# A block recurrence inside a two-layer decoder trunk: the output part of each block is moved and cut up, its last block gets an order of its own, and one norm is shortened

## The reference

```python
def step(S, w_t, k_t, v_t, a_t, b_t, r_t):          # RWKV-7, per token
    sa = S @ a_t
    S = S * w_t + outer(sa, b_t) + outer(v_t, k_t)
    return S, S @ r_t
o = (o - mean(o)) * rsqrt(mean((o - mean(o))**2) + GN_EPS)   # per head
o = (o * lnx_w + lnx_b + bonus) * g

def step(S, q_c, k_c, u_c, w_c, g_c, qk_c):         # gated DeltaNet, per chunk of 64
    v_new = u_c - w_c @ S
    o_c = (q_c * exp(g_c)) @ S + qk_c @ v_new
    S = S * exp(g_last) + (k_c * exp(g_last - g_c)).T @ v_new
    return S, o_c
o = o * rsqrt(mean(o * o) + RMS_EPS) * norm_w * silu(z)      # per head
```

## Time and profile before

| | us |
|---|---|
| median of 3 runs | 1497.6 |
| profiled execution, its own time | 1500.85 |
| its span, first to last instruction | 1499.0 |
| PE busy | 1442.7 (96%) |
| DVE (VectorE) busy | 665.2 (44%) |
| ACT (ScalarE) busy | 597.8 (40%) |
| POOL (GpSimd) busy | 520.8 (35%) |
| granted PE clock, mean | 0.995 |

### The profile page before, as it was taken

One profiled execution on the slowest core, in us unless ns is written; L12 is line 12 of the kernel. 1 busy time (PEld: TensorE's weight loads), 2 busy tenths in 40 slices (PEclk: granted clock), 3 DMA queues, 4 the chain that ended last, 5 costly groups with the idle time before them and its releaser, 6 DMA issues.

```text
span 1499.0 us, 24712 instructions
## 1 busy us (share of the span) xinstructions
PE 1442.7 (96%) x10353; PEld 1147.0 (77%) x10353; DVE 665.2 (44%) x1100; ACT 597.8 (40%) x848; POOL 520.8 (35%) x234
## 2 busy tenths in 40 slices
PE   7999998887899999999999999999999999999998
PEld 5787678787768788888888677785587888888886
DVE  4675656778653412214133528856633314132231
ACT  5524663434354422223132444667744223132231
POOL 3543332101024434434335232331244434334341
PEclk9999999999999999999999999999999999999999
DMA  4333200000112232322323212220022322322321
GB/s 144 85 98 85 70 15 3 3 3 3 59 57 85 85 112 84 110 87 84 112 84 92 78 58 83 85 85 1 2 84 85 104 92 84 113 84 87 105 88 56
DMA packets 128393, 110.01 MB, mean 73 GB/s; under 512 B 10678, under 2 KB 126512, under 8 KB 128304
## 3 DMA queue, kind: packets, MB, share of 16 engines
q1 hardware_dynamic: 127712, 107.64, 23.2%
q10 hardware_dynamic: 592, 1.07, 0.2%
HBM read 106.60 MB, written 2.10 MB: 73 GB/s over the span
## 4 chain that ended last, share of the span: by engine, by line
PE 89%; DVE 5%; ACT 3%; POOL 1%; issue 1%; DMA 1%; ACTq 0%; SPq 0%; DVEq 0%; POOLq 0%
PE ps L535 23%; PE ps L530 23%; PE ps L531 23%; PE ps L667 5%; PE ps L991 1%; PE ps L1001 1%; PE ps L1012 1%; PE ps L682 1%; PE ps L567 1%; PE ps L966 1%; POOL pw_lo L2067 1%; PE ps L675 1%; PE ps L644 1%; PE ps L771 1%; PE ps L942 1%
## 5 line engine op out<-in xcount | busy, mean ns | idle before, releaser
L2146 POOL TENSOR_TENSOR w_lo<-lower,w_hi 128x2048 fp32r<-128x2048 f32 (+1 forms) x84 | 389.1, 4632 | 612.2 <-ACT w_hi L1093 612.2
L530 PE MATMUL ps<-h_hi,w_hi 128*128 128x512 f32 x792 | 315.5, 398 | 2.3 <-ACT h_hi L1098 1.6
L531 PE MATMUL ps<-h_hi,w_lo 128*128 128x512 f32 x792 | 312.1, 394 | 0.0
L1093 ACT ACTIVATE w_hi<-lower 128x2048 fp32r<-128x2048 f32 (+1 forms) x84 | 160.2, 1907 | 242.8 <-PE ps L535 242.8
L535 PE MATMUL ps<-h_lo,w_hi 128*128 128x512 f32 x792 | 202.0, 396 | 0.5
L530 PE MATMUL ps<-a_hi,w_hi 128*128 128x512 f32 x480 | 189.1, 394 | 0.0
L531 PE MATMUL ps<-a_hi,w_lo 128*128 128x512 f32 x480 | 189.1, 394 | 0.0
L530 PEld LDWEIGHTS ps<-h_hi,w_hi 128*128 128x128 f32 x792 | 148.6, 188 | 44.5 <-issue 6.9
L535 PEld LDWEIGHTS ps<-h_lo,w_hi 128*128 128x128 f32 x792 | 148.7, 188 | 38.0 <-DVE h_lo L1655 2.5
L531 PEld LDWEIGHTS ps<-h_hi,w_lo 128*128 128x128 f32 x792 | 148.7, 188 | 35.5 <-issue 1.2
L1898 DVE TENSOR_TENSOR lower<-lower,ps 128x512 f32<-128x512 f32 x64 | 44.0, 687 | 268.5 <-PE ps L535 268.5
(11 more groups left out here) (364 smaller groups left out, 1913.9 us busy)
## 6 DMA issues: line engine op xcount, KB each, us to landing
lower<-in_mlp_w_dram SPq DMA_DIRECT2D x64, 1024.0 KB, 5.4
lower<-in_ev_w_in_dram SPq DMA_DIRECT2D x30, 512.0 KB, 3.8
lower<-in_od_w_in_dram SPq DMA_DIRECT2D x10, 1024.0 KB, 5.1
lower<-in_ev_w_out_dram SPq DMA_DIRECT2D x4, 1024.0 KB, 5.2
lower<-in_od_w_out_dram SPq DMA_DIRECT2D x4, 1024.0 KB, 5.0
out_dram<-lower SPq DMA_DIRECT2D x4, 512.0 KB, 3.2
lower<-in_od_w_in_dram SPq DMA_DIRECT2D x6, 256.0 KB, 3.8
upper<-in_x_dram SPq DMA_DIRECT2D x1, 1024.0 KB, 7.8
```

Source lines behind the costliest of these rows:

```text
L530: pe.matmul(o, wh, xh, start=(i_ == 0), stop=False)
L531: pe.matmul(o, wl, xh, start=False, stop=False)
L1093: act.activation(WH[:, u % 2, :, 0:w], RAW[:, u % 2, :, 0:w], ACT.Copy).then_inc(hi_ready, 1)
L2146: pool.tensor_tensor(WL[:, u % 2, :, 0:w], RAW[:, u % 2, :, 0:w], as_f32(WH[:, u % 2, :, 0:w]), ALU.subtract)\
```

## The change

1. The loop has four turns; turn 4 is gone, and block 3 gets a list of its own.
2. In turns 1 and 2 the output part is spread out. VectorE does only the three sums after level 1 (`chunk_out`, results now in PSUM banks 6 and 7 in place of OR and OG), the mean and its subtraction (`centred`, two operations where there were three) and `decay_steps` after level 2, `out_var` (two reductions, without the two small scalings, which ScalarE's Ln now has as scale and bias) and `scaled_rows` after level 3, and `out_scaled` after level 4. ScalarE squares after its copies of level 3 and does Ln and Exp after those of level 4. `turned_out` of block m comes in turn m + 2, on PE between `state_reads` and `scaled_inputs`, on ScalarE ahead of its copies of BTOK and KTOK; `mixed` comes in turn m + 2 after level 0.
3. In all turns the mask that makes QIR is issued before RBM, in place of after RK; and `state_reads` scales the state part in place in PSUM.
4. Turn 3 keeps the output of block 2 whole, and has `mixed(2)` at its end. It also does, before its level 4 products, the first half's `state_reads` of block 3 and the reads for its output (into banks 2 and 3, which are spare), and VectorE the operations that follow.
5. The end (block 3): RK times VR starts the output in bank 2; the second half's sums follow the first half's in bank 2 and bank 7; ScalarE splits the last copy in two; a dummy Ln of four columns comes between the halves; GpSimd scales QSS; `weight_hi(0)` comes after both halves; GQ is finished before R, by one operation each from PSUM, and its tiles are copied and multiplied first (`MIXED`). `keep_busy` falls from 17 matmuls to 6.
6. `norm(2)`: VectorE adds only squares 1 to 5, and PE takes the sum and squares 6 and 7 with three matmuls; the two `keep_busy` ahead are gone; a dummy Ln stands after square 6; `weight_hi(u_ikv + 1)` comes after the eight copies, and GpSimd's part of it waits for the low parts.

```diff
@@ PE
+                for k in range(KT - 2, KT):
+                    pe.wait_ge(squares, KT * (n - 1) + k + 1)
+                    mm = pe.matmul(o[:, :], ONES, SQ[n][:, k, :], start=False, stop=(k == KT - 1))
...
+                if s > 1:
+                    turned_out(s - 2)
                 scaled_inputs(s)
...
+                if s == TT - 1:
+                    pe.wait_ge(r_mkv, TT)
+                    state_reads(s, 0)
+                    last_reads(s, 0)
                     turned_out(m)
+                joined_blocks(s, LAST - 1)
+            s = TT - 1
+            pe.wait_ge(r_rs, 2 * s + 1)
+            both_halves(LAST_OR, RK[s], VR[s % 2], True)
+            pe.wait_ge(r_tr, s)
+            pe.wait_ge(r_tg, s)
+            pe.wait_ge(inv_done, 2 * s + 2)
+            last_chunk(s, 0)
+            state_sums(s, 0, False)
+            half_added(0, LAST_OR, RBM[s], UN)
+            state_reads(s, 1)
+            last_reads(s, 1)
+            last_chunk(s, 1)
+            pe.wait_ge(r_u, 2 * s + 2)
+            half_added(1, LAST_OR, RBM[s], UN).then_inc(f_or, 1)
+            one_half(0, 7, GRK[s], VN)
+            pe.wait_ge(r_y, 2 * s + 2)
+            one_half(1, 7, GRK[s], VN).then_inc(f_og, 1)
+            keep_busy(bank[3], 5)
@@ ACT
+            last_solved(0)
+            act.activation(UNUSED, ONES[:, 0:4], ACT.Ln)
+            last_solved(1)
+            weight_hi(0)
+            last_squares()
+            out_rms(TT - 1)
@@ DVE
             def lower_products(s):
                 dve.wait_ge(r_lt, s + 1)
+                dve.tensor_tensor(QIR[s % 2], LTR, mask(MERGE[:, 0, :]), mul).then_inc(inv_m, 1)
...
+            def centred(o):
+                t.link(dve.tensor_reduce(NMEAN, o.rearrange("p (h v) -> p h v", h=NH), AX.X, add, negate=True))
+                o = o.rearrange("p (h v) -> p h v", h=NH)
+                dve.scalar_tensor_tensor(out=o, in0=per_row(NMEAN), scalar=1.0 / HD, in1=o, op0=mul, op1=add)\
+                   .then_inc(e_oc, 1)
...
+                if s > 1:
+                    mixed(s - 2)
                 joined_blocks(s, 1)
                 if behind:
                     chunk_out(m)
+                if s == TT - 1:
+                    centred(bank[6])
+                joined_blocks(s, 2)
+                if s == TT - 1:
+                    out_var(m)
+                elif behind:
+                    centred(bank[6])
                 if s < TT - 1:
                     decay_steps(s + 1)
+                joined_blocks(s, 3)
+                if s == TT - 1:
                     out_scaled(m)
+                    state_reads(s, 0)
+                else:
+                    if behind:
+                        out_var(m)
+                    scaled_rows(s + 1)
+                joined_blocks(s, 4)
                 if s < TT - 1:
+                    if behind:
+                        out_scaled(m)
+                else:
+                    solved(s, 0)
                     mixed(m)
+                    state_sums(s, 0)
+            state_reads(s, 1)
+            last_out()
+            out_var(s)
+            out_scaled(s)
+            last_mixed()
```

More of the change, by code:

```diff
@@ L780, in state_sums, with half_added, last_reads, last_chunk @@
                 outer(5, KGT[s % 2], VN, True).then_inc(f_sg, 1)
+            def half_added(k, b, mats, vals):
+                part = HALVES[k]
+                for h_ in range(NH):
+                    j, q = h_ // 2, h_ % 2
+                    mm = pe.matmul(ps[part, b, h_ * HD:(h_ + 1) * HD], mats[part, j, q, :], vals[part, j, q, :],
+                                   start=False, stop=True, skip_group_check=True)
+                return mm
+            def last_reads(s, k):
+                by_state(s, k, 0, R, SR, SPARE[k])
+                by_state(s, k, 4 * HD, GQ, SG, SPARE[k]).then_inc(f_qs, 1)
+            def last_chunk(s, k):
+                c = 2 * s + k
+                pe.wait_ge(r_x1, c + 1)
+                one_half(k, 6, QIR[s % 2], X1R).then_inc(f_u, 1)
+                pe.wait_ge(r_ks, c + 1)
+                one_half(k, 7, QIG[s % 2], VG[s % 2]).then_inc(f_y, 1)
             def chunk_out(s):
@@ L793, in turned_out @@
                 turn(7, OG.rearrange("p j q v -> p j (q v)"), f_tg)
[L795 to L798, removed]
+            for s in range(TT):
+                m, behind = s - 1, s > 0
+                turned_inputs(s)
                 if behind:
                     state_reads(m, 0)
[L801 to L804, removed]
+                if s > 1:
+                    turned_out(s - 2)
+                scaled_inputs(s)
@@ L820, in _ @@
+                below_blocks(s, 0)
+                joined_blocks(s, 0)
                 if behind:
[L821 to L825, removed]
                     state_sums(m, 1)
-                if behind:
                     chunk_out(m)
[L829 to L833, removed]
@@ L834, in _ @@
-                if not ahead:
-                    keep_busy(bank[3], 10)
-                if behind:
-                    turned_out(m)
[L838 to L841, removed]
+                for lev in range(1, LAST - 1):
+                    below_blocks(s, lev)
+                    joined_blocks(s, lev)
+                below_blocks(s, LAST - 1)
+                if s == TT - 1:
+                    pe.wait_ge(r_mkv, TT)
+                    state_reads(s, 0)
+                    last_reads(s, 0)
+                    turned_out(m)
```

256 lines of the change are left out of this document (149 added, 107 removed).

## The result

The changed kernel takes 1490.95 us, the median of 20 runs (1476.23 to 1498.91). The kernel before takes 1500.13 beside it (1497.57 to 1504.3). The ratio is 0.9928, with a 95% interval of 0.9913 to 0.9943: 9.2 us gained. The forecast was 1475.0, a gain of 22.55, and its range ended at 1484. The ratio leaves out the slowest of the 20, 1498.91. The direction was right, the size less than half of the forecast. The profiled execution took 1491.00 (span 1489.2), so nothing hangs on an offset between it and the median.

A forecast was written before the change was run, and what follows sets the result against it. PE work was taken as 89% of the span, with gains only where PE waits or runs at half clock. Turn, end and norm terms summed to 22.55 us: 1500.85 becomes 1478.3, less 3.25 for the median, 1475.0; range 1469 to 1484.

The forecast's parts named there:

- Levels of turns 1 and 2, 3.75 and 5.2: Inverse levels: spreading DVE's output part starts them earlier, gaining 3.75 us in turn 1 and 5.2 in turn 2.
- `turned_out` 0.9, `out_scaled` free: Before the inverses of turns 2 and 3, `turned_out` costs 0.9 us each; `out_scaled` at a turn's end costs nothing.
- Turn 0, +0.75: Turn 0: the early QIR mask removes the transpose's wait for GpSimd, gaining 0.75 us.
- The end, 13.6, and the norm, 2.4: Last inverse to projection: 13.6 us gained (bounds 9 and 15); norm's shorter chain: 2.4 (bounds 1 and 3.2).
- It costs 0.45 in turns 1, 2 and 3 (bounds 0 and 0.69): QIR mask ahead of the key mask in DVE's list: its 0.69 us product costs 0.45 in each turn.
- I take the clock as kept: Between inverse levels: remaining idle pieces of 0.6 to 1.1 us are under half of 2.83, so PE keeps full clock.
- The clock falls at the end: Rival: with 6 of 17 fillers left, PE idles and loses clock once or twice: 1476.5 to 1478, chance 0.11.
- the clock stays low into the projection: Rival: low clock kept through the output projection; 60 us low cost 30, giving 1505; chance 0.03.
- The levels pay nothing: Rival: DVE's work only moves between inverse levels and stays later than PE; gains shrink to 1 each: 1482, chance 0.12.
- out_scaled waits: Rival: Ln and Exp end 1.5 to 2 us later, shifting turns 2 and 3: +3.5, 1478.5, chance 0.11.
- One load: Rival, from the skill's rule that one table set holds Ln and Exp: two times 1.28 less, 1472.5, chance 0.04.
- the three that were to prove it wrong: Turn 2's levels no closer than 5 us; PE waiting for ScalarE's `turned_out` before turns 2 and 3; end over 24 us.

The follow-up runs named there:

- experiment 5: Kernel of experiment 2 with the output part of turns 1 and 2 as it was before the change: 1485.41 us, ratio 0.9891.
- experiment 1: Changed kernel with the QIR mask back behind RK, all else as changed: 1479.65 us, ratio 0.9866 against the kernel before.
- experiment 3: Changed kernel with both the QIR mask back behind RK and two filler matmuls in PE's wait for RK: 1478.6 us, ratio 0.9845.
- experiment 9: Kernel of experiment 2 with the norm as it was before the change: 1480.14 us, ratio 0.9858.
- Experiment 4: Kernel before with only the QIR mask moved ahead of RBM: 1509.93 us, ratio 1.0062.
- experiment 2: Changed kernel, mask still early, with two filler matmuls in PE's wait for RK: 1477.37 us, ratio 0.9838 against the kernel before.
- experiment 6: Kernel of experiment 1 with the mask of MK done twice, so that RK comes later; no filler: 1500.17 us, ratio 0.9977.
- experiment 7: Kernel before with two filler matmuls in PE's wait for RK: 1502.48 us, ratio 1.0001.
- experiment 10: Kernel of experiment 2 with one filler matmul in place of two: 1481.14 us, ratio 0.9858.
- experiment 11: Changed kernel, QIR mask early in turn 0 alone; two filler matmuls in turn 0's RK wait, one in other turns, more at other waits: 1475.16 us, ratio 0.9838.

## Why the prediction was wrong

Point by point, by its own steps:

- *Levels of turns 1 and 2, 3.75 and 5.2:* right. The four start times are within 0.13 us of the trace, the gains there are 3.93 and 5.25, and experiment 5 gives 7.5 for what the terms put at 7.15.
- *`turned_out` 0.9, `out_scaled` free:* right; the front of turn 2 is 0.97 longer than that of turn 1 in experiment 1 (31.67 for 30.70), and the decays started at 1.62 for 1.65.
- *Turn 0, +0.75:* turn 1 begins at 250.78 in place of 251.64, 0.86 earlier, although the clock was low for 3.4 us longer in turn 0 of this execution. Where turn 0 kept its clock, it took 33.29 with the mask late (experiment 3) and 32.38 with it early (experiment 9), 0.9 less.
- *The end, 13.6, and the norm, 2.4:* the norm gave 2.4. The end gave 12.0 by the trace (32.6 less 19.65, less 0.92 for the reads ahead of level 4), so this term was 1.6 too high. The end alone was in no run. By subtraction, 23.9 less 7.5 less 2.4, 14.0 is left for the end, turn 0 and the mask, for which the forecast's terms give 13.0 (13.6 + 0.75 - 3 x 0.45).
- *"It costs 0.45 in turns 1, 2 and 3 (bounds 0 and 0.69)":* this is the step that failed. (Its sum is loose too: 0.69 less the 0.16 to spare is 0.53.) The direct delay of 0.67 in turn 1 was inside the bounds. What was outside is that a longer idle of PE is a risk for the clock, whose price is paid in the 10 us that follow. The front's 4.45 in turn 1 (35.02 for 30.57) holds 0.67 of delay; nearly all the rest is the low clock. Experiment 4 puts 8.7 us on this one move in the kernel before; experiments 1 and 2 put 12.4 and 14.7 (by the gains) on it or on its idle in the changed one. Over all three turns the fronts of the profiled execution are 14.99 us longer than before, where 3.15 was forecast. With the mask back (experiment 1) they are 2.3 longer, the mask's delay adds some 2.1, and 10.6 is left for the clock.
- *"I take the clock as kept":* argued from the idle pieces between levels, where it held. I had the price list in hand (2.83 idle, and the next 64 matmuls at half rate) and used it for the levels and the end only. The front had a wait of 1.5 to start from; with 0.69 more in it, it stood nearer to 2.83 than anything else in the turn, and three times over. The trace of the kernel before even held a fall with no idle piece over 1.5 us ahead of it, in turn 0, which the prediction doesn't mention. Timeline of PE and a window, kernel before:

```profile
227.22 1.15 PE L667 MATMUL ps<-upper,lower 64*64 64x64 f32 x32 [1.50 <-DVE upper L1713]
...
229.81 3.60 PE L667 MATMUL ps<-lower 64*64 64x64 f32 x64 [1.45 <-DVE lower L1725]
```

```profile
230.00:232.00 2.00, 2.00 (x42) 2.00 (x42) 0.00 (x0) 0.25 (x1) 0.02 (x1) 0.50 0.00 0
```

The profiled executions close the account: of the 22.55 forecast, 9.8 came. The fronts are 11.8 of the missing 12.7 and the end 1.6; the levels, turn 0 and what differs elsewhere gave back 0.7.

Of the rivals, none was this one. "The clock falls at the end" and "the clock stays low into the projection" had the mechanism at the wrong place: at the end it stayed at 1.00. "The levels pay nothing" and "out_scaled waits" are refuted by the timeline. "One load" too: the table load between Ln and Exp is still there (422.77), 1.28 us as before, against the rule that was weighed. That the kernel would be faster was right. The range was too narrow, for it left out a fall of the clock three times in a row. Three of the signs that it named failed: turn 1 took 50.42 for 46.6, turn 2 51.23 for 47.4, and turn 2's clock was not 1.00. None of the three that were to prove it wrong came, since none of them watched the front's clock.

Open: what decides, at one and the same wait, whether the clock falls (experiment 6: in front of turn 1, not of turns 2 and 3), and why it still falls for 3.4 us in one front where the wait is filled (turn 3 in experiments 2, 3, 7 and 9, turn 1 in experiment 10, turn 2 in experiment 11); how much of what experiment 6 costs beyond the QIR mask is its front of turn 0; which executions lose it behind the norm (experiment 1); and the 4 to 6 us by which runs of one kernel still differ at clocks of 0.995 to 1.000.

## What to carry to other kernels

When an edit lengthens a wait of TensorE, cost the clock behind it and not the wait alone: look in the windows for what the engine did around every idle piece that grows, also one that an edit of 0.7 us on another engine touches, and compare its new length with the shortest idle in the trace that was followed by a low clock. No length parted safe from unsafe here: growing a wait from 1.5 to 2.2 us made falls frequent and long, but 2.24 went without one and 1.13 with one. Where the wait can't be shortened, two filler matmuls in it are a cheap test, and here they were worth 13.6 us, though they did not rule a fall out. If the runs of a kernel spread more than those of the one before, put their granted clocks beside their times before looking at any instruction.

## What the runs showed of the hardware

- An idle piece of 2.2 us in front of groups of 64x64 matmuls was followed by about 10 us at 1.2 GHz (265 to 275); one of 1.5 at the same place was not, in the kernel before and in experiment 1. Neither holds each time: 2.24 was not followed by a fall in turns 2 and 3 of experiment 6, and idle pieces of 1.50 and 1.45 were, for 3.4 us, in turn 0 of the kernel before. I had expected such a fall to be short while PE is busy, as after 2.83 idle in turn 2 of the kernel before. In that stretch PE has many small idle pieces: the window 268 to 270 has it busy 1.12 of 2 in the kernel after. The Trainium skill, "TensorE: Matmul & The Clock Gate", section "A second HAM failure mode: psum-queue depth-cycling", describes frequent short idles between groups of matmuls that make the clock swing between its levels; the windows here agree in kind.
- The fall is not the same in each execution: one program gave 1476 to 1499 (clock 0.997 to 0.980), another 1483 to 1504.
- An operation of VectorE with two SBUF inputs, 128x256, took 0.68 when it started beside GpSimd's last 0.40 us and 0.42 with GpSimd idle (L1831 in the kernel after, the same operation L1756 before).
